# Two expert layers: where the late rows' residual, norm and queries stand in the order of the picks

## What is computed

```python
h = h + g1 * y                                   # residual of the mixer before
a = rms_norm(h, g_norm2) * (1 + scale) + shift   # the layer's input
q = (a @ w_query).reshape(128, 8, 2, 128)        # 8 heads, two halves
s = einsum("thpd,hpnd->thpn", q, sub_keys)       # 128 scores for each half
s_top, i_top = top_k(s, 16)
cand = s_top[:, :, 0, :, None] + s_top[:, :, 1, None, :]
best, pos = top_k(cand, 16)                      # 16 experts of 16384 for each token and head
gate = softmax(best)
act = gelu(einsum("thkd,td->thk", u_tab[expert], a))
out = einsum("thk,thkd->td", gate * act, v_tab[expert])
```

## Time and profile before

| | us |
|---|---|
| median of 3 runs | 3023.45 |
| lowest, highest | 3022.43, 3026.78 |
| profiled execution, its own time | 3026.27 |
| its span, first to last instruction | 3024.5 |
| busy: TensorE, VectorE, ScalarE, GpSimd | 2634.0, 1957.1, 1110.3, 633.8 |
| first gather issued, layer 0 and layer 1 | 342.24 and 1203.79 |

### The profile page before, as it was taken

How to read it: one execution, slowest core, us unless ns; L and a number is a source line. 1 busy time by engine, 2 the same in 40 slices (tenths; PEclk the granted TensorE clock), 3 DMA queues, 4 the chain that set the end, 5 groups by cost and what they waited for, 6 DMA issues and landing times. The chain is left out here.

```text
span 3024.5 us, 36176 instructions
## 1 busy us (share of the span) xinstructions
PE 2634.0 (87%) x11546; PEld 1734.7 (57%) x11546; DVE 1957.1 (65%) x4771; ACT 1110.3 (37%) x2635; POOL 633.8 (21%) x600
## 2 busy tenths in 40 slices
PE   7989888878877697888887787899989999999998
PEld 4534743333332387543333332898849989985798
DVE  1866467776676596777776775666746666675565
ACT  3245332222222312322222221545545454454544
POOL 0400144434444200354443542000000000000000
PEclk9989999999989898999999989899989999999999
DMA  8940799999999833999999999555415545542454
GB/s 301 384 158 1 292 369 418 416 420 411 412 416 418 340 102 131 377 414 418 413 416 420 407 412 398 180 183 166 153 66 174 183 159 187 186 151 77 146 184 149
DMA packets 152950, 832.41 MB, mean 275 GB/s; under 512 B 17008, under 2 KB 17136, under 8 KB 86384
## 3 DMA queue, kind: packets, MB, share of 16 engines
q0 software_dynamic: 85392, 579.38, 46.8%
q1 hardware_dynamic: 65664, 238.65, 23.5%
q10 hardware_dynamic: 1760, 12.70, 1.2%
HBM read 829.61 MB, written 1.05 MB: 275 GB/s over the span
## 5 line engine op out<-in xcount | busy, mean ns | idle before, releaser
L1719 PE MATMUL ps<-arena 128*128 128x512 f32 x2016 | 964.9, 627 | 251.6 <-ACT arena L1128 251.4
L1719 PEld LDWEIGHTS ps<-arena 128*128 128x128 f32 x2016 | 383.0, 198 | 823.4 <-ACT arena L1128 427.5
L2342 DVE SCALAR_TENSOR_TENSOR arena<-arena 128x1024 f32<-128x1024 f32 x512 | 626.4, 1225 | 330.6 <-DMA arena<-experts,arena 330.2
L815 POOL DMA_INDIRECT arena<-experts,arena x512 | 577.6, 1128 | 1090.5 <-PE ps L1719 721.1
L2075 DVE TENSOR_TENSOR w_lo<-weights,w_hi 128x512 fp32r<-128x512 f32 x528 | 364.6, 691 | 284.4 <-ACT w_hi L895 283.9
L1128 ACT ACTIVATE arena<-con,arena 128x128 f32<-128x128 f32 x504 | 203.0, 403 | 749.1 <-DVE arena L2349 749.1
L895 ACT ACTIVATE w_hi<-weights 128x512 fp32r<-128x512 f32 x528 | 332.9, 631 | 384.9 <-PE ps L1661 285.1
L1659 PE MATMUL ps<-a_hi,w_hi 128*128 128x256 f32 x1408 | 400.5, 284 | 3.1 <-DVE a_lo L2088 1.6
L1660 PE MATMUL ps<-a_lo,w_hi 128*128 128x256 f32 x1408 | 399.1, 283 | 0.0
L1661 PE MATMUL ps<-a_hi,w_lo 128*128 128x256 f32 x1408 | 399.1, 283 | 0.0
L1659 PEld LDWEIGHTS ps<-a_hi,w_hi 128*128 128x128 f32 x1408 | 270.6, 192 | 9.2 <-issue 2.2
(11 more groups left out here) (272 smaller groups left out, 3114.2 us busy)
## 6 DMA issues: line engine op xcount, KB each, us to landing
weights<-stream SPq DMA_DIRECT2D x453, 512.0 KB, 3.5
arena<-mod_rows_in POOLq DMA_DIRECT2D x71, 512.0 KB, 9.2
arena<-experts,arena POOLq DMA_INDIRECT x512, 15.7
mod_rows<-mod_rows_in POOLq DMA_DIRECT2D x9, 512.0 KB, 8.5
arena<-gain_rows ACTq DMA_DIRECT2D x1, 3072.0 KB, 12.3
arena<-rpb_windows ACTq DMA_DIRECT2D x4, 512.0 KB, 15.2
arena<-keys_in ACTq DMA_DIRECT2D x2, 1024.0 KB, 7.4
arena<-tab_mix ACTq DMA_DIRECT2D x2, 768.0 KB, 4.3
```

Of the source, the lines that this page charges most:

```text
L815: pool.indirect_dma_start(out=pair_ring[:, k % PAIR_RING, :], out_offset=None, in_=experts[l], in_offset=bass.IndirectOffsetOnAxis(ap=expe ...
L1719: ins = pe.matmul(ps[:, 2 * b + half, :], diag[:, k % DIAGS, :], v_part[:, k % PAIR_RING, HALF * half:HALF * (half + 1)], start=(k == TOPK ...
L2342: dve.scalar_tensor_tensor(out=u, in0=u, scalar=1.0, in1=h_rows[:, b, :], op0=ALU.mult, op1=ALU.mult, accum_out=act_raw[:, k:k + 1]).then_ ...
```

## The change

- `late_add` of all eight chunks moves from ahead of the loop to round 1 (`LATE_SUM_AT`) on VectorE; the squares, now one instruction over 8x128 elements, to round 1 on ScalarE; the sums to round 1 on TensorE, ahead of values 1.
- The root, the scaling, the shift and `first_head(1)` move to round 3 (`LATE_NORM_AT`). The scaling on VectorE is one multiplication by the root over all chunks; the gain goes into ScalarE's shift instruction as its scale.
- Selections 1 and 2 move from picks 3 and 9 to 6 and 12. Queries of head 1 and 2 move from picks 2 and 6 to 6 and 11.
- Each head's queries and keys become three pieces (tile one, tile two, keys) at its pick n, n + 2 and n + 4. ScalarE copies a piece one round after TensorE's round.

The diff, cut to its core:

```diff
@@ constants
-CHOOSE_AT = {3: 1, 9: 2, **{PER_CHOICE * i: i + TB for i in range(1, CHOICES - TB)}}
-QUERY_AT = {2: 1, 6: 2, **{PER_HEAD * (h - LEAD) + PER_CHOICE: h for h in range(LEAD, H)}}
+LATE_SUM_AT, LATE_NORM_AT = 1, 3
+CHOOSE_AT = {6: 1, 12: 2, **{PER_CHOICE * i: i + TB for i in range(1, CHOICES - TB)}}
+QUERY_AT = {6: 1, 11: 2, **{PER_HEAD * (h - LEAD) + PER_CHOICE: h for h in range(LEAD, H)}}
+PIECE_AT = {n + 2 * part: (h, part) for n, h in QUERY_AT.items() for part in range(3)}
...
@@ ScalarE
-                wait_product(act, pl["late"][1])
-                square_chunks(f"late{l}", lambda c: act.wait_ge(late_added, KC * l + c + 1))
-                root(pl["late_norm"], f"late{l}")
-                shift(f"late{l}", lambda c: a_in[:, c, block_cols[1]], lambda c: mod[:, l, 24 + c, 0:1])
-                first_head(1, pl["query"][0], pl["keys"][0])
+
+                def late_squares():
+                    wait_product(act, pl["late"][1])
+                    act.wait_ge(late_added, KC * (l + 1))
+                    act.activation(a_in[:, :, block_cols[1]], h_res[:, :, block_cols[1]], ACT.Square).then_inc(chunk_squared, KC)
+
+                def late_norm():
+                    root(pl["late_norm"], f"late{l}")
+                    act.wait_ge(scaled_ready, FEEDS[f"late{l}"])
+                    for c in range(KC):
+                        x = a_in[:, c, block_cols[1]]
+                        act.activation(x, x, ACT.Identity, bias=mod[:, l, 24 + c, 0:1],
+                                       scale=gain[:, (2, 4)[l], c:c + 1]).then_inc(a_ready, 1)
+                    first_head(1, pl["query"][0], pl["keys"][0])
+
                 for n in range(GROUPS):
...
+                    if n == LATE_SUM_AT:
+                        late_squares()
+                    if n == LATE_NORM_AT:
+                        late_norm()
                     if n in CHOOSE_AT:
                         gate_exps(CHOOSE_AT[n])
-                    if n in QUERY_AT:
-                        query(QUERY_AT[n])
-                        keys(QUERY_AT[n])
+                    if n - 1 in PIECE_AT:
+                        piece(*PIECE_AT[n - 1])
...
@@ TensorE
-                    for c in range(KC):
-                        sum_chunk(pl["late_norm"], f"late{l}", c)
...
-                first_head(1, pl["t_query"][0:2], pl["query"][0], pl["keys"][0], f"late{l}")
                 for n in range(GROUPS):
-                    if n in QUERY_AT:
-                        query(QUERY_AT[n])
-                        keys(QUERY_AT[n])
+                    if n == LATE_SUM_AT:
+                        for c in range(KC):
+                            sum_chunk(pl["late_norm"], f"late{l}", c)
+                    if n == LATE_NORM_AT:
+                        first_head(1, pl["t_query"][0:2], pl["query"][0], pl["keys"][0], f"late{l}")
+                    if n in PIECE_AT:
+                        piece(*PIECE_AT[n])
                     values(n)
...
@@ VectorE
-                for m in range(KC):
-                    late_add(m)
-                normed(f"late{l}", pl["late_norm"], 1)
+
+                def late_normed():
+                    key = f"late{l}"
+                    r = inverse(key, pl["late_norm"])
+                    dve.tensor_tensor(a_in[:, :, block_cols[1]], h_res[:, :, block_cols[1]],
+                                      r.unsqueeze(1).to_broadcast([P, KC, P]), ALU.mult).then_inc(scaled_ready, KC)
+
                 for n in range(GROUPS):
...
+                    if n == LATE_SUM_AT:
+                        for m in range(KC):
+                            late_add(m)
+                    if n == LATE_NORM_AT:
+                        late_normed()
                     if n in CHOOSE_AT:
                         choose(CHOOSE_AT[n])
```

More of the change, by code:

```diff
@@ L304, in peer, with piece @@
         a["t_query"] = plan.tiles(2 * H)
[L305 to L314, removed]
+        a["keys"] = [None] * H
+        a["query"] = [[None, None] for _ in range(H)]
+        def piece(h, part):
+            if part < 2:
+                a["query"][h][part] = plan.product(a["t_query"][2 * h + part])
+            else:
+                a["keys"][h] = plan.product()
+        for part in range(3):
+            piece(0, part)
         a["rows"] += [plan.product() for _ in range(2)]
         for n in range(GROUPS):
-            if n in QUERY_AT:
-                query(QUERY_AT[n])
-                keys(QUERY_AT[n])
+            if n in PIECE_AT:
+                piece(*PIECE_AT[n])
         a["back"] = [plan.product() for _ in range(4)]
@@ L1095, in peer, with piece @@
                 shift(key, lambda c: a_in[:, c, block_cols[0]], lambda c: mod[:, l, 24 + c, 0:1])
[L1097 to L1101, removed]
+                def piece(h, part):
+                    if part < 2:
+                        pr = pl["query"][h][part]
+                        copy_product(pr, pq[:, h % LEAD, part, :], bank(pr)[:, 0:T])
+                        return
                     if h >= LEAD:
@@ L1695, in peer, with piece @@
                 base = PICKS * l
-                def query(h):
-                    for t, pr in zip(pl["t_query"][2 * h:2 * h + 2], pl["query"][h]):
+                def piece(h, part):
+                    if part < 2:
+                        t, pr = pl["t_query"][2 * h + part], pl["query"][h][part]
                         claim(pr)
                         linear(t, bank(pr)[:, 0:T], lambda k: a_in[:, k, :]).then_inc(tile_done[t.unit], 1)
-                def keys(h):
+                        return
                     pr = pl["keys"][h]
```

## The result

The changed kernel took 3034.76 us (median of 20 runs, 3029.39 to 3047.12), the kernel before 3031.3 in 20 runs beside it (one of which took 8744.68 and does not count in the ratio). The ratio is 1.0023, 95% interval 1.0013 to 1.0033: slower, by about 7 us. Of the 11.3 us between 3034.76 and the 3023.45 from which the forecast was made, 7.9 are thus the reference's own: it ran longer here than in its first three runs. The profiled execution of the changed kernel took 3029.39, its span is 3027.6.

A forecast was written before the change was run, and what follows sets the result against it. DMA engines were taken as the bound, with 16.2 us of holes to win. Losses of 6 and 7 us made the profiled 3026.27 into 3039.3, which, standing 2.8 above the median, gave 3036 us; range 3029 to 3045.

The forecast's parts named there:

- The likeliest case: Whole kernel: the change makes it slower, 3036 us named, 3029 to 3045 as range, chance 0.62.
- the hole at gather 19: Layer 0, 405 to 412: low DMA stretch replaced by ones around 416 to 424 and 434 to 441.
- +6 in layer 0, +7 in layer 1: Expert layers: loss of 6 us in layer 0 and 7 in layer 1, sum 13 us.
- Late norm at pick 3: Between picks 3 and 4: late head takes 7 us, ScalarE free at 376.0, values 3 run 376.5 to 378.2.
- The clock: TensorE's slow 1.2 GHz level, given to values 0 and 12; unknown by 1.7 us either way per layer.
- First dots ahead: Layer 0 start: weighing 0 comes at 356.9 instead of 361.20, values 0 end at 361.0 instead of near 365.
- rival 1: Gathers 19 to 22: the DMA holes close, faster; full closing 3007 us, half 3015; chance 0.25.
- the most the change can give: Both expert layers: 16.2 us lost while DMA engines are short of work, the ceiling on any gain.
- Beyond pick 40: Rest of each layer: selections and pieces 32 picks apart, covered by ten queued gathers, costed at nothing.
- the wash: Both layers: TensorE at full clock, head 6.5 us, loss 0 to 3 us each, 3018 to 3029; chance 0.13.
- Rival 3: Late norm: ScalarE held until 379 rather than 376, each layer loses 10 us, 3044; chance 0.08 within slower cases.
- Rival 4: Layer start: dot 0 moves by at most 2.2 us, dot 1 not at all; already in the sum, no chance given.

The follow-up runs named there:

- e5: The kernel before, unchanged, run once more for a second profile; ratio 0.9997.
- e3: The kernel before with only selections 1 and 2 moved to picks 6 and 12 and whole queries of heads 1 and 2 to 6 and 11; ratio 0.9963.
- e9: The kernel before with only the due picks changed, the same program as e3, once more on another chip; ratio 0.9941.
- e2: The changed kernel with whole queries and keys at the due picks instead of pieces, late work still behind the first dots; ratio 1.0006.
- e11: The changed kernel with whole queries instead of pieces, the same program as e2, run again in a later group; ratio 0.9955.
- e6: The changed kernel, unchanged, run once more beside the kernel before on one chip; ratio 1.0020.
- e1: The changed kernel with late residual, squares, norm and head put back ahead of the loop, pieces and due picks kept; ratio 1.0028.
- e10: The kernel before with the due picks and the late norm as one multiplication and eight shifts with gain, still ahead of the loop; ratio 0.9939.
- e12: The kernel before with the due picks and ScalarE copying a whole query one pick later; ratio 0.9944.
- e4: The changed kernel with the table set holding both logarithm and exponential named ahead of the late root; ratio 1.0054.
- e7: The kernel before with selections 1 and 2 at picks 4 and 10, heads 1 and 2 at 2 and 8, queries copied one pick later; ratio 0.9933.

## Why the prediction was right, and what it had wrong

The parts add up (layers, us, both layers together):

| | early form | late form |
|---|---|---|
| kernel before | 1333.6 | 1348.7 (e5) |
| + due picks | 1323.2 (e3), -10.4 | 1330.5 (e9), -18.2 |
| + late work moved | 1336.3 (e2), +13.1 | 1337.5 (e11), +7.0 |
| + pieces | 1358.4 (after), +22.1 | 1357.5 (e6), +20.0 |
| total | +24.8 | +8.8 |

How firm these sums are: the two kernels profiled twice in a form that doesn't differ came out within 1.2 us of themselves (after and e6, e2 and e11). From gather 40 to 255 all fourteen profiles take 1104 to 1109 us in both layers together, so nearly all of each difference is made by gather 40. The measured times of the late groups say the same: due picks -0.0059, the move +0.0014, pieces +0.0065 (e6 less e11), which are -18, +4 and +20 us.

Theory B holds with A as the lesser part: the pieces cost about 21 us, the move 7 to 13. e1 agrees (due picks and pieces without the move: +10.6 = -10.4 + 21.0). Two small parts are inside these steps: the move brings the one multiplication with it, which by the ratio of e10 is worth nothing, and the pieces bring ScalarE's later copy, which by e12 is worth nothing. The two lines above the total are kernels whose dot 0 comes alike in all profiles; each stands beside the reference of its column. The changed kernel itself was not run in the first group; e4 there, with 1359.7, stands in for it. The time of 3034.76 was taken where before runs at 3031, which is the late form by its time, and the ratio of 1.0023 (7 us) is near the +8.8. e4, where before ran at 3017, came out at 1.0054 (16 us).

**The forecast, point by point.** The likeliest case (slower, 3029 to 3045, 3036 named) came true; that the time came within 1.3 us of the one named is luck (below). Right in kind were: the hole at gather 19 moved to 22 and 26; gather 19 was issued earlier than before and 22 and 26 later; values 3 stood behind the late head, with ScalarE held.

The term "+6 in layer 0, +7 in layer 1" was mis-sized for the form of the start whose rows it was worked out from. Against the kernel before as its first profile shows it, gather 29's issue fell back by 12.2 us, and each layer by 12.3 and 12.5. In relation to gather 0 the working went wrong in these places:
- *Late norm at pick 3.* ScalarE was forecast free 33.8 us after gather 0 and was at 35.0; values 3 started at 35.5, not 34.3. The third table load (1.28) and the longer shift (0.7) were not in it; values 0 ending early gave some of that back. The multiply, taken at the nearest row's 1.22, took 1.23. The head took 364.66 to 372.53, 7.9 us, where I took 7.
- *The clock.* It was given to values 0 and 12 alone. Values 6 and 7 idled behind selection 1 for 4.48 us and took 6.48 where 3.7 was due; values 16 and 17 took 5.40. That selection 1 with one piece leaves TensorE idle follows from my own figures, 9.2 less 3.5; I had given the slow clock for such idling behind selection 2 only. Gather 16 was forecast at 50.0 and came at 53.8, gather 22 at 75.2 and 79.3, gather 26 at 92.9 and 98.2. The 1.2 us of the head, 2.8 of picks 6 and 7 and 1.7 of picks 16 and 17 make 5.7 of the 6.3 us by which layer 0 was forecast too short; that is an estimate from these rows.
- *First dots ahead.* Values 0 ended 17.6 us after gather 0, forecast 18.8. Right.
- *Due picks.* The sum never priced them alone. They gain 10 to 18 us, which is close to rival 1's "holes close", and the pieces then give it back. The 18 is more than the 16.2 us that the prediction called the most the change can give; that ceiling was read from the early form, whose layers are 15 us shorter. The forecast named half of each piece lying outside the selection as the cost; that was the right mechanism. The clock is the other part: set against full-clock records, picks 6 and 7 lost 6.48 - 3.71 = 2.8 us, pick 12 3.64 - 1.99 = 1.7 and picks 16 and 17 5.40 - 3.71 = 1.7, together 6.1 and at most that of the layer's loss, as the kernel before has slow stretches too (0.67 from 404 to 414).
- *Beyond pick 40.* From pick 40 to 60 the changed kernel takes 60.9 us against 56.8, and by the last pick it has them back (552.0 for picks 40 to 255 against 552.8). Right in sum. All kernels with the later copy show this shift (e7 and e12 too, which have no pieces).

Why the number came out all the same: the kernel before loses 15 us more in its layers where the start has the late form, and the changed one doesn't. That was not in the forecast. It makes the change cost 8.8 us in the layers and 7 by the ratio, where 24.8 stands against the rows used and 13 was forecast; and it goes with a reference of 3031.3 in place of 3023.45. A loss forecast some 6 us too large on a start 7.9 us too low gave nearly the right time. The mechanism was right in kind, the sizes met by luck.

**The rivals.** The full closing of the holes and the wash did not come. Rival 3 (ScalarE held to 379, 10 us a layer) had the size per layer nearly right, by another cause: ScalarE was held 1.2 us longer, and the rest was clock and pieces. Rival 4's bound held against the first profile (dot 0 at 8.8 us after gather 0 instead of 10.6, 1.8 earlier, with 2.2 as the most), except that dot 1 moved too, from 13.5 to 12.2.

**The rule of the Trainium skill.** After the load at 359.37 for 1.28 the logarithm starts at 360.67, and after the load at 361.05 the exponential starts at 362.34: no pause, and none ahead of a load either (the diagonal ends at 372.93, the load starts at 372.95), so the trace again doesn't show the drain of about 1.38 us that the Trainium skill, ScalarE: Activation LUTs, "What ACT_TABLE_LOAD costs", adds to each switch.

**What stays open.** Why the start has two forms, and what exactly is late in it. With the work ahead of the loop, the traces of the early form give the landing times of all gathers, those of the late form of none (e12 of 50), so the form goes with the chip or the way the profile was taken.

Why the unchanged parts differ between profiles: behind layer 1 from 1143.6 to 1154.5 us; between the layers 194.7 once and 187.0 to 189.9 in all others. They differ for one and the same kernel too (behind layer 1 before took 1154.0 and 1148.0, e2 and e11, the same program, 1144.0 and 1150.3), and the granted clock goes with it: 0.99 where that part took 1143.6 to 1144.0, 0.97 where it took 1153.8 to 1154.5. The changed kernel had the short form in both its profiles. Those were its fastest execution of 20 and its second of 12, so they say little of its usual run: by the medians of e5 and e6 the change costs 8.5 us, as by the layers (8.8), and the times show nothing given back. The first pair of profiles alone, with its 21.7 us, would have called the change nearly free.

How the pieces' cost divides into open work and clock is an estimate. The late work was not moved without the due picks.

## What to carry to other kernels

When long work is cut into pieces to be gentle on a queue, count how much of each piece no longer runs beside another engine's long work: a whole query under a selection was hidden, and the same query in pieces cost some 10 us a layer, partly as work in the open and partly because the idling TensorE fell to its lower clock level. Try the parts of a combined change one by one; here the smallest edit (four due picks in two tables) was the gain and the other two were the loss. And take a second profile of the reference beside the change, since what the first one shows of a wait may be only one of its forms.

## What the hardware showed that was not expected

- A logarithm followed by an exponential loaded two table sets, 1.28 us each (359.37 and 361.05), until the set that holds both was named ahead (e4: one load).
- The same program's layer start varied by 6.6 us (dot 0 at 10.6 or at 17.2 us after gather 0) from profile to profile, with a wait whose releaser the trace doesn't name, and the kernel's median was 3017 in the group whose profiles with the late work ahead had the early form, and 3030 in the two groups with the late one (3023 in the first three runs, whose profile had the early form). That the one makes the other fits the layers' lengths and wasn't shown by itself.
- After 3.62 us of work and 4.48 us of idling the next eight value records of TensorE took 6.48 us, with a granted clock of 0.50 in the first 3.2 us (e1: 6.48 after 4.98 idle), where eight took 3.71 at full clock; after 7.07 us of work, the keys and 0.98 us of idling four took 1.99 (e3).
